# Three moves in the instruction order of a two-block float32 program: rotations in two steps, retention's low parts ahead of two weight splits, two half loads of an expert issued earlier

## The reference

```
z = rms_norm(x, g) @ w_in                 # 1024 -> 3200 columns
rq, rk, rv, rg, aq, ak, av, gu, gv = split(z)
rq, rk, aq, ak = apply_rope(...)          # t*cos + rotate_half(t)*sin, 6 heads of 64 each
y_ret = silu(rg) * retention(rq, rk, rv)  # group-normalised
y_att = dilated_attention(aq, ak, av)
y_gm  = spatial_gating(gelu(gu), gelu(gv))
x = x + rms_norm(concat(y_ret, y_att, y_gm) @ w_out, g2)
x = x + rms_norm((silu(gate) * up) @ w_down, g3)
```

## Time and profile before

| | |
|---|---|
| median of 3 runs | 1585.37 us (1584.95 to 1586.96) |
| the profiled execution | 1586.37 us |
| its span, all engines | 1584.6 us |
| TensorE (PE) busy | 1547.1 us, 98% |
| VectorE (DVE) busy | 877.9 us, 55% |
| ScalarE (ACT) busy | 614.1 us, 39% |
| GpSimd (POOL) busy | 262.6 us, 17% |
| HBM read | 407.72 MB |

### The profile page before, as it was taken

One profiled execution on the slowest core, in us unless ns is written; L12 is line 12 of the kernel. 1 busy time (PEld: TensorE's weight loads), 2 busy tenths in 40 slices (PEclk: granted clock), 3 DMA queues, 4 the chain that ended last, 5 costly groups with the idle time before them and its releaser, 6 DMA issues.

```text
span 1584.6 us, 23758 instructions
## 1 busy us (share of the span) xinstructions
PE 1547.1 (98%) x9598; PEld 1177.3 (74%) x9598; DVE 877.9 (55%) x1441; ACT 614.1 (39%) x1111; POOL 262.6 (17%) x224
## 2 busy tenths in 40 slices
PE   8999999999999999999999999999999999999997
PEld 6889999778889998888777888998544444444542
DVE  6655447456466885678778776466433333333323
ACT  4654444346554444555457665343211111111110
POOL 2341222002322210000037662010200000000000
PEclk9999999999999999999999999999999999999998
DMA  8643977537429986333527767858999999999994
GB/s 298 212 155 127 300 260 249 204 117 246 150 84 300 299 280 234 98 81 83 156 84 203 209 175 249 256 160 314 376 405 425 421 421 424 422 422 425 421 421 197
DMA packets 204212, 410.49 MB, mean 259 GB/s; under 512 B 6981, under 2 KB 150929, under 8 KB 182720
## 3 DMA queue, kind: packets, MB, share of 16 engines
q1 hardware_dynamic: 197104, 379.08, 66.7%
q10 hardware_dynamic: 3584, 19.86, 3.1%
q0 software_dynamic: 3408, 9.95, 1.8%
HBM read 407.72 MB, written 1.15 MB: 258 GB/s over the span
## 4 chain that ended last, share of the span: by engine, by line
PE 85%; DMA 7%; DVE 5%; ACT 1%; issue 1%; POOL 0%; SPq 0%; DVEq 0%; ACTq 0%; POOLq 0%
PE ps L144 83%; DMA arena<-in_w_expert_up 2%; DMA arena<-in_w_expert_gate 2%; PE ps L146 2%; DVE arena L150 2%; DVE split_r L150 1%; DVE arena L154 1%; DMA ring<-in_w_out 1%; DMA cst_sb<-in_cst 1%; ACT split_r L148 1%; DMA ring<-in_w_in 1%; ACT arena L148 0%; POOL stat L150 0%; DVE arena L152 0%; DVE X L154 0%
## 5 line engine op out<-in xcount | busy, mean ns | idle before, releaser
L144 PE MATMUL ps<-arena_r,split_r 128*128 128x256 f32 (+1 forms) x2984 | 457.4, 288 | 0.1
L144 PEld LDWEIGHTS ps<-arena_r,split_r 128*128 128x128 f32 x2984 | 392.9, 188 | 13.4 <-issue 7.3
L150 DVE TENSOR_TENSOR split_r<-ring,split_r 128x1024 fp32r<-128x1024 f32 (+1 forms) x245 | 291.7, 1204 | 191.3 <-ACT split_r L148 190.3
L148 ACT ACTIVATE split_r<-ring 128x1024 fp32r<-128x1024 f32 (+1 forms) x293 | 296.5, 1019 | 236.6 <-PE ps L144 175.6
L144 PE MATMUL ps<-split_r,arena_r 128*128 128x512 f32 (+1 forms) x1520 | 341.6, 378 | 4.8 <-DVE split_r L150 2.9
L144 PEld LDWEIGHTS ps<-split_r,arena_r 128*128 128x128 f32 x1520 | 276.0, 189 | 51.5 <-issue 9.3
L144 PE MATMUL ps<-arena 128*64 128x512 f32 (+8 forms) x1232 | 301.5, 469 | 3.1 <-DVE arena L160 1.7
L144 PE MATMUL ps<-ring,arena 128*64 128x512 f32 (+2 forms) x688 | 226.4, 576 | 2.6 <-DMA rows<-in_w_expert_gate 1.0
L144 PE MATMUL ps<-hhh_r,split_r 128*128 128x256 f32 (+1 forms) x976 | 228.4, 322 | 0.0
L144 PEld LDWEIGHTS ps<-arena 128*64 128x64 f32 (+2 forms) x1232 | 120.5, 150 | 112.2 <-issue 103.5
L150 DVE TENSOR_TENSOR arena<-arena,ps 128x512 f32<-128x512 f32 (+1 forms) x132 | 81.1, 641 | 204.3 <-PE ps L144 168.3
(11 more groups left out here) (163 smaller groups left out, 1289.0 us busy)
## 6 DMA issues: line engine op xcount, KB each, us to landing
ring<-in_w_gate_up SPq DMA_DIRECT2D x44, 1024.0 KB, 7.7
ring<-in_w_in SPq DMA_DIRECT2D x57, 512.0 KB, 5.4
arena<-in_w_ada SPq DMA_DIRECT2D x24, 1024.0 KB, 5.8
arena<-in_w_expert_gate SPq DMA_DIRECT2D x12, 2048.0 KB, 26.4
ring<-in_w_down SPq DMA_DIRECT2D x22, 1024.0 KB, 4.9
ring<-in_w_expert_up SPq DMA_DIRECT2D x11, 2048.0 KB, 25.0
ring<-in_w_expert_down SPq DMA_DIRECT2D x11, 2048.0 KB, 27.3
ring<-in_w_in SPq DMA_DIRECT2D x28, 768.0 KB, 5.5
```

The lines of the kernel that those rows point to most:

```text
L144: made = e.matmul(*a, **k)
L148: made = e.activation(*a, **k)
L150: made = e.tensor_tensor(*a, **k)
```

## The change

First, the four subtractions and additions of `rotated` become a function of their own, `rotated_sums`, and stand one step later in VectorE's loop, behind the low part of that step: unit 0 in steps 1 and 2, unit 1 in 4 and 5, unit 3 in 12 and 13, unit 4 in 16 and 17. Second, at the end of a layer's mixing half, `y_low` of retention moves ahead of `lo_to(n0 + 36)`, which makes the low parts of the last two quarters of the output projection. Third, the two half loads of expert load 3 are issued with groups 0 and 1 of branch b in place of groups 2 and 3.

```diff
@@ ScalarE, gates
-                    if u >= 2:
+                    if u < 2:
                         s.wait_ge(*at("ba", 3))
-                        half_load(s, 3, u - 2)
+                        half_load(s, 3, u)
@@ VectorE, rotated
                     then(v.tensor_tensor(fold(Z[:, i, c0:c0 + 384], 12), bk, cos, ALU.mult), ("rot1", l, u, i))
+
+            def rotated_sums(l, u):
+
+                c0 = Z_UNITS[u][0]
                 for i in range(2):
                     z2 = Z[:, i, c0:c0 + 384].rearrange("p (a c b) -> p a c b", c=2, b=32)
@@ VectorE, loop of the layer
                     if k == 1:
                         rotated(l, 0)
+                    if k == 2:
+                        rotated_sums(l, 0)
                     if k == 4:
                         rotated(l, 1)
+                    if k == 5:
+                        rotated_sums(l, 1)
...
                         rotated(l, 3)
+                    if k == 13:
+                        rotated_sums(l, 3)
                     if k == 16:
                         rotated(l, 4)
+                    if k == 17:
+                        rotated_sums(l, 4)
@@ VectorE, end of the mixing half
-                lo_to(n0 + 36)
                 for i in range(2):
                     y_low("ret", 5, 3, i)
+                lo_to(n0 + 36)
                 weighed("pr", j, 0)
```

## The result

The changed kernel takes 1589.78 us, the median of 12 runs (1588.39 to 1591.93); the kernel before, run beside it on the same chip, 1585.71 us (12 runs, 1583.51 to 1587.17). The medians lie 4.1 us apart. The ratio, taken over all runs, is 1.0028, with a 95% interval of [1.0019, 1.0036]: by it the changed kernel is 4.4 us slower (3.0 to 5.7). The forecast was 1584.5 us and no change that the times can tell; the result lies 3.2 us above the top of the range. The profiled spans are 1584.6 us before and 1589.2 after.

A forecast was written before the change was run, and what follows sets the result against it. TensorE, busy 98% of the span, was taken as the bound, so only its stalls or low clock could pay. Terms +0.3 + 2 x 0.15 - 1.15 - 0.4 = -0.95 us gave 1584.5 us, range 1582.1 to 1586.6.

The forecast's parts named there:

- The rotations, unit 4: Sums run after VectorE's pause, so the copy of retention's keys slips 0.45 us: +0.15 us per layer, bounds 0 and +0.6.
- The rotations, units 0 and 1: The low-part stall goes but returns at transposes and scores: layer 1 0, layer 0 +0.3 us.
- Unit 3: Rotation sums come 0.9 us later where VectorE is idle at times and the transposes have over 1 us: 0.
- The low parts of retention: Output projection: PE starts 0.77 us sooner behind `y_low`, gives back 0.2: -0.57 us per layer, -1.15 together.
- The half loads: Stall at the output weights in the last block shortens by 2.3 - d: -0.4 us, bounds -2.4 and +1.7.
- d: Delay of the worse of two loads, branch b's last or output weights' first, beside a half load: taken as 1.9 us.
- the row of 4.9 us: Earlier landing, undelayed, with the half load 1.06 us behind; a sign that d may be small.
- The clock: Fall to 1.2 GHz behind the stall at 1093, costing about 1.7 us; a change in it was not counted in the sum.
- the split of the rotations pays: Rival: both first stalls go and do not come back, -1.4 us in place of +0.3: 1582.8 us; chance 0.1.
- the half loads only trade places, and lose: Rival: half loads drain first at both places, d = 4 costs +1.7 us: 1586.5, or 1588.2 with a clock fall; chance 0.15.
- The loads come free: Rival: d small, stall at 1093 closes, no clock fall remains: 1581.8 us, or 1582.4 without a median fall; chance 0.15.
- Nothing reaches the end: Rival: the expert stream decides the end, so PE's gains before 1120 us are eaten: 1585.4 us; chance 0.1.

The follow-up runs named there:

- experiment 3: The whole change, with GpSimd made to wait for unit 4's rotated heads before one low part in each layer: 1585.37 us, 1.0002 to the kernel before.
- experiment 5: The kernel before with only the sums of units 0 and 1 moved a step later: 1585.33 us, ratio 0.9994.
- Experiments 1: The changed kernel with unit 4's four sums put back behind their products: 1584.68 us, ratio to the kernel before 0.9998.
- experiment 10: The kernel before with retention's low parts ahead, half loads behind the output weights' last high part, and idle multiplications filling the routing: 1582.8 us, ratio 0.9975.
- experiment 8: The kernel before with both half loads moved behind the last high part of the output weights: 1583.99 us, ratio 0.9987.
- 9: The kernel before with retention's low parts ahead and the half loads behind the last high part of the output weights: 1582.99 us, ratio 0.9976.
- 7: The kernel before with only the two half loads issued early: 1586.1 us, ratio 0.9997.
- 11: The kernel before with only 7 and 3 more idle TensorE multiplications in the routing: 1582.08 us, ratio 0.9967.

## Why the prediction was wrong

**The rotations, unit 4: the step that failed.** The text said that the sums "used to run in that pause and now come after it, 1.3 us lost to VectorE", and put +0.15 us in each layer, with +0.6 as the bound. It measured 2.19 us in each layer. The prediction walked down VectorE's queue with the durations of the old place, 1.29 us for the sums among them, and never put GpSimd's timeline beside the new one. The needed rows were there: a low part on GpSimd of 2.40 us from 69.97, and sums that would now run from about 69.07 (67.84 + 1.23) to 70.36. They overlap in the last of the four. And what an overlap costs stood in the same trace, seven times, at 865 to 956 us. Without the overlap the step was sound: experiment 3 has the slip of the copy at 0.45 us and PE at +0.14 and +0.13 us. That it fits to the hundredth is partly chance, since 0.11 of the 0.45 us are a low part on VectorE that met the end of GpSimd's, which that experiment itself had put later. Nor did any rival name the overlap; the one that ended slower was about DMA.

**The rotations, units 0 and 1: right in size, and right in kind.** "The stall comes back between" is what experiment 5 shows in layer 1, and layer 0 lost its 0.3 us. In the changed kernel's own profile layer 1 lost 1.09 us there; ScalarE waited for a load of `w_in` that took 5.53 us to land instead of 4.43. Experiments 1, 3 and 5 have the same order and -0.09, -0.17 and +0.03 us, so that was the execution; experiment 10, which does not split these units, has +0.57 us there. What nobody gains by the split is the lesson of the row of 13.22 busy us in 13.5: where the engine that is waited for has no idle time, its order only decides at which instruction one waits.

**Unit 3:** no step of the delay lies there: 0, as predicted.

**The low parts of retention: right.** Predicted -0.77 sooner, 0.2 given back, -0.57 in a layer; measured -0.75, +0.24 and -0.52.

**The half loads: a term mis-sized, too small to see in the times.** The text had the half load issued 0.2 us behind the last load of branch b, and put d, what the worse of the two loads beside a half load is delayed, at 1.9 us. In the profiles the half load goes out from 0.37 us ahead of that load to 0.02 us behind it. The last load of branch b landed 2.3 to 3.3 us later than its 5.1 to 5.4, in all five profiles with early half loads. By the prediction's own formula, 2.3 less that delay, the gain of 0.4 us becomes nothing or a small loss, and the times say 0.9997. The second half load followed the first load of output weights by 1.0 to 1.1 us in four of the five, not by 0.5, and that load landed in 5.5 to 6.4 us against 5.3 to 6.0: there the hint of the row of 4.9 us in the earlier trace rows held, nearly. The stall itself was 2.07 us, not 2.4, by the three kernels in which it is gone, and it varies by 2 us between executions. What closes it is to let the half loads follow the last needed transfer (experiment 8).

**The clock:** the prediction counted a fall behind the stall at 1093, since its one profile had one. That was a rare place: of the profiles of the changed kernel and the twelve experiments none has it there. The usual place without filler is the routing: 8 of 10 such profiles (the changed kernel and experiments 1 to 9) show a fall at 1111 to 1120 us, of 3.4 or 6.8 us, none of the three with filler, and experiments 3 and 7 are the two without. Four of the ten (the change, 1, 5 and 9) have a second one of 3.4 us at 1539 to 1546, which adds 1.7 us to PE's delay and which the prediction left out too.

**The other rivals:** "the split of the rotations pays" fell with experiment 5. Of "the half loads only trade places, and lose" the trade is what the landings show, and the loss of 1.7 us is not: its d = 4 measured 2.3 to 3.3. "The loads come free" fell with the same landings. "Nothing reaches the end" is refuted by the result: what two layers lost before 411 us is in the time at the end. Experiments 8, 9 and 11, whose intervals exclude 1, show it for gains.

**The sum put right:** -0.95 with 2 x 2.19 in place of 2 x 0.15 is +3.1 us, and with a gain of 0.4 us by the half loads left out +3.5. Measured is +4.4 (3.0 to 5.7 by the interval), so the corrected sum lies within.

## What to carry to other kernels

A duration in a trace belongs to its neighbours as much as to its instruction: before moving a VectorE instruction with both inputs in SBUF, lay GpSimd's timeline under the new place. An instruction of 0.35 us that starts just behind a GpSimd one of 2.4 us costs 2.5 us, and one wait on GpSimd buys it back. Look in the trace for like instructions of very unlike length: the price stood there, 2.22 us beside 0.43, before anything was moved. And before a stall of 1 to 2 us is worth an edit, see in several executions of the same code that it is there.

## What the runs showed of the hardware

- VectorE against GpSimd: of four like instructions only the one that started after GpSimd was held, and to its end plus 0.22 us; GpSimd kept its 2.37 us. When GpSimd started 0.04 us behind VectorE (741.99 in the kernel before), GpSimd was held. In experiment 3 VectorE's next low part, two inputs in SBUF too, met the tail of GpSimd's at 72.44 and took 1.34 us in place of 1.23; GpSimd ended at 72.71. In three cases of different size the held instruction ended at GpSimd's end plus its own usual time less 0.13 to 0.16 us: 72.41 for 72.19 + 0.35, 73.78 for 72.71 + 1.23, and 868.00 for 867.72 + 0.43.
- Waits of PE of 1.8 and 0.9 us in the routing were followed by a fall from 2.4 to 1.2 GHz in most profiles and not in others, with the same code there; a fall lasted 3.4 or 6.8 us. With waits cut to 0.21 and 0.27 us by filler it came in none of three. The Trainium skill (TensorE: Matmul & The Clock Gate, What's actually happening) calls the count behind it free-running; that the same code has the fall in one execution and not in the next agrees.
- A load of 0.5 or 1 MB landed 2 to 3 us later when a half load of 1 MB was issued between 0.37 us ahead of it and 0.08 us behind it (7.1 to 8.4 us in ten of ten cases, against 4.7 to 5.4 without), and no later when the half load came 0.39 us behind (4.9 us, one case).
- Two half loads of 1 MB moved behind the loads that PE waited for closed a stall of 1.92 us in three profiles of three, and the 35 us after 1120 then had 401 to 420 GB/s in place of 355.
